# Taking one step of look-ahead and two row buffers out of a software-pipelined attention loop

## The reference

```
p = softmax(q k^T * scale + bias, causal)      # per head, 128 queries at a time
o = p v
```

## Time and profile before

| | us |
|---|---|
| median of 3 runs | 2262.34 |
| lowest, highest | 2261.17, 2263.99 |
| profiled execution, its own time | 2263.99 |
| its span in the trace | 2262.7 |
| PE busy | 2133.4 (94%) |
| DVE, ACT, POOL busy | 988.6, 815.3, 226.7 |

### The profile page before, as it was taken

The page is one execution under the profiler, slowest core; times in us unless marked ns, Lnnn a source line. Parts: engine busy times, 40 slices in busy tenths (PEclk is TensorE's granted clock), DMA queues, the critical chain, the costliest instruction groups (busy, mean ns, idle before and its releaser), DMA issues. The chain is left out here.

```text
span 2262.7 us, 25574 instructions
## 1 busy us (share of the span) xinstructions
PE 2133.4 (94%) x10364; PEld 1712.6 (76%) x10364; DVE 988.6 (44%) x1833; ACT 815.3 (36%) x1574; POOL 226.7 (10%) x256
## 2 busy tenths in 40 slices
PE   6899899999998999999999999988898999999997
PEld 5667688888887767688888877767665788888886
DVE  6265453323336364453323346645355444333333
ACT  4145443223224355342222334342355434222222
POOL 3003410000000004210000000000254201000000
PEclk9899999999999999999999999989899999999999
DMA  6521123233332312123333222313411232323321
GB/s 154 109 75 57 57 80 106 89 98 103 93 98 71 94 47 75 62 84 97 98 98 93 98 80 75 93 29 84 103 48 38 61 117 84 102 89 101 100 89 69
DMA packets 273721, 192.10 MB, mean 85 GB/s; under 512 B 22060, under 2 KB 241364, under 8 KB 273604
## 3 DMA queue, kind: packets, MB, share of 16 engines
q1 hardware_dynamic: 268704, 177.76, 27.3%
q0 software_dynamic: 4752, 12.67, 2.5%
q10 hardware_dynamic: 148, 0.04, 0.0%
HBM read 186.21 MB, written 4.23 MB: 84 GB/s over the span
## 5 line engine op out<-in xcount | busy, mean ns | idle before, releaser
L584 PE MATMUL bank<-h_features,weights_hi_lo 128*128 128x512 f32 (+1 forms) x5160 | 1138.2, 381 | 17.1 <-DVE weights_hi_lo L917 7.9
L584 PEld LDWEIGHTS bank<-h_features,weights_hi_lo 128*128 128x128 f32 x5160 | 933.7, 190 | 206.7 <-issue 14.6
L917 DVE TENSOR_TENSOR weights_hi_lo<-weights,weights_hi_lo 128x1024 fp32r<-128x1024 f32 (+1 forms) x337 | 402.7, 1199 | 703.7 <-ACT weights_hi_lo L1521 703.1
L1521 ACT ACTIVATE weights_hi_lo<-weights 128x1024 fp32r<-128x1024 f32 (+1 forms) x337 | 340.9, 1016 | 401.2 <-PE bank L626 352.4
L624 PE MATMUL bank<-weights_hi_lo,hidden 128*128 128x512 f32 x528 | 205.4, 389 | 0.0
L625 PE MATMUL bank<-weights_hi_lo,hidden 128*128 128x512 f32 x528 | 205.4, 389 | 0.0
L626 PE MATMUL bank<-weights_hi_lo,hidden 128*128 128x512 f32 x528 | 205.4, 389 | 0.0
L1637 ACT ACTIVATE hidden<-arena 128x512 fp32r<-128x512 f32 x66 | 41.7, 632 | 300.0 <-DVE arena L1068 300.0
L1930 POOL TENSOR_SCALAR arena<-arena,row_stats 128x256 f32<-128x256 f32 (+5 forms) x140 | 126.3, 913 | 198.7 <-DVE row_stats L992 70.9
L1902 POOL TENSOR_TENSOR h_features<-arena,h_features 128x512 fp32r<-128x512 f32 x24 | 30.7, 1278 | 992.0 <-ACT h_features L1549 992.0
L1068 DVE TENSOR_TENSOR arena<-bank,arena 128x512 f32<-128x512 f32 x66 | 45.6, 692 | 181.3 <-PE bank L584 181.3
(11 more groups left out here) (335 smaller groups left out, 2063.8 us busy)
## 6 DMA issues: line engine op xcount, KB each, us to landing
weights<-in_w_in_dram SPq DMA_DIRECT2D x84, 512.0 KB, 3.9
weights<-in_w_gate_dram SPq DMA_DIRECT2D x66, 512.0 KB, 3.8
weights<-in_w_up_dram SPq DMA_DIRECT2D x66, 512.0 KB, 3.8
weights<-in_w_down_dram SPq DMA_DIRECT2D x60, 512.0 KB, 3.6
weights<-in_w_out_dram SPq DMA_DIRECT2D x24, 512.0 KB, 3.7
bias_rows<-decay_scratch POOLq DMA_DIRECT2D x16, 256.0 KB, 4.0
weights<-in_w_cmp_dram SPq DMA_DIRECT2D x16, 256.0 KB, 5.4
weights<-in_w_down_dram SPq DMA_DIRECT2D x12, 256.0 KB, 2.6
```

The source lines that it names most:

```text
L584: last = e.matmul(out_ap, l, r, start=(j == 0), stop=(j == len(pairs) - 1))
L917: e.tensor_tensor(pair_view(i, 1), raw_view(i), pair_view(i, 0).bitcast(F32), ALU.subtract).then_inc(done, tick(("split", i)))
L1521: e.activation(pair_view(i, 0), raw_view(i), ACT.Copy).then_inc(done, tick(("hi", i)))
```

## The change

`LAG`, the number of iterations after the last step, goes from 6 to 5. The transposes of a step and their copies come two iterations after its scores instead of three, the values and their output one iteration earlier too. The row buffers shrink from eight to six, so a step reuses the rows of step i-3. `HEAD_AT` and `HEAD_OUT_AT` move one iteration earlier; the other fills stay at their iterations. The same edit is made in the loops of all engines.

```diff
-LAG = 6
-HEAD_AT = {4 * h + 10: h for h in range(N_DIFF)}
-HEAD_OUT_AT = {4 * h + 22: h for h in range(N_DIFF)}
+LAG = 5
+HEAD_AT = {4 * h + 9: h for h in range(N_DIFF)}
+HEAD_OUT_AT = {4 * h + 21: h for h in range(N_DIFF)}
...
-        ATTN_E = [arena(12288 + 512 * i, T) for i in range(6)] + [arena(16384, T), JUNK[:, :]]
+        ATTN_E = [arena(12288 + 512 * i, T) for i in range(6)]
...
-        NSA_E = [arena(8192 + 512 * i, T) for i in range(6)] + [arena(12288, T), TOK_WORDS[:, 1024:1536]]
+        NSA_E = [arena(8192 + 512 * i, T) for i in range(6)]
...
-                        if 3 <= i <= n + 2:
-                            turn_weights(steps[i - 3], [rows[(2 * (i - 3) + j) % 8] for j in range(2)])
-                        if i - 4 in groups:
-                            weigh_values(groups[i - 4])
+                        if 2 <= i <= n + 1:
+                            turn_weights(steps[i - 2], [rows[(2 * (i - 2) + j) % 6] for j in range(2)])
+                        if i - 3 in groups:
+                            weigh_values(groups[i - 3])
...
-                                    if i >= 4:
-                                        dve.wait_ge(*row_free(steps[i - 4], j))
+                                    if i >= 3:
+                                        dve.wait_ge(*row_free(steps[i - 3], j))
...
-                        if i - 5 in groups and groups[i - 5].final:
-                            g = groups[i - 5]
+                        if i - 4 in groups and groups[i - 4].final:
+                            g = groups[i - 4]
```

More of the change, by code:

```diff
@@ L965, in attend @@
                     n = len(steps)
-                    row = lambda i, j: rows[(2 * i + j) % 8]
+                    row = lambda i, j: rows[(2 * i + j) % 6]
                     for i in range(n + LAG):
@@ L1000, in attend @@
                         fill(i)
-                        if 3 <= i <= n + 2:
-                            u = steps[i - 3]
+                        if 2 <= i <= n + 1:
+                            u = steps[i - 2]
                             for j in range(len(u.turned)):
@@ L1564, in attend @@
                                 if u.bias is None:
-                                    if i >= 4:
-                                        act.wait_ge(*row_free(steps[i - 4], j))
+                                    if i >= 3:
+                                        act.wait_ge(*row_free(steps[i - 3], j))
                                     bank = banks[*u.name, "s", j]
@@ L1591, in attend @@
                                     banks.leave(act, (*u.name, "turned", j))
-                        if i - 4 in groups and groups[i - 4].final:
-                            g = groups[i - 4]
+                        if i - 3 in groups and groups[i - 3].final:
+                            g = groups[i - 3]
                             if s == "M" or g.tile >= N_DIFF:
@@ L1928, in attend @@
                                 for j in range(2):
-                                    row = rows[(2 * (i - 1) + j) % 8][:, 0:u.w]
+                                    row = rows[(2 * (i - 1) + j) % 6][:, 0:u.w]
                                     e.tensor_scalar(row, row, st[:, 6 + j:7 + j], None, ALU.mult).then_inc(done, tick((*u.name, "scaled", j)))
```

## The result

The changed kernel takes 2301.2 us (median of 4 runs, 2294.0 to 2307.5) against 2262.9 (4 runs, 2261.2 to 2264.0): it is 38 us slower and not 13, the direction as forecast and the time outside the range. The ratio is 1.0162, interval 1.0135 to 1.0190; it takes in three more runs of the changed kernel (2295.1, 2297.2 and the profiled one, 2303.4), so by it the loss is nearer to 37 us. The profiled execution of it spans 2302.1 us, 39.4 more than the one before.

A forecast was written before the change was run, and what follows sets the result against it. The prediction took PE, busy 94% of the span, to bound the kernel. It added 11.2 us for M and 2.2 for L0 and L1, 13.4 in all, to the median of 2262.3: 2275.7 us, range 2262 to 2285.

The forecast's parts named there:

- the total, 11.2 + 2.2: Whole kernel: 11.2 us lost in M plus 2.2 in L0 and L1, 13.4 us slower, 2275.7 us.
- The second mis-sized term: Loops of L0 and L1: a loss of 1.1 us a layer, 2.2 in both.
- Row buffers at nothing: Six row buffers instead of eight: the wait for a free row is always over when reached, cost 0.
- M's idle time: M's loop: 3.2 + 4.6 + 0.5 + 0 at repeating gaps, 1.3 at its beginning, 1.6 at its end, 11.2 us.
- Kinds B and C: M's iterations 8, 20, 32, 44 (B: new gap replaces old, cost 0) and 12, 24, 36 (C: loss 3.2 us).
- Kind A: M's iterations 4, 16, 28, 40: transposes wait 1.2 us more for POOL's rows, four times, 4.6 us in sum.
- The signs: Trace checks: M's transposes wait 8 to 14 us for POOL, M's loop some 170 us, L0's 160; clock under 0.88 means wrong.
- the third rival: M's clock falls more often, seven more slow stretches of 1.5 us, 2287 us; or row buffers are scarce; chance 12%.
- T(10): Transposes of step 10 in L0 and L1, at iteration 12 between two fills: wait 1.8 us for a mix on DVE.
- The drain: L0 and L1 after the last fill: last scores end 4.2 us later, following chain 8.3 instead of 11.6, loss 0.9.
- Rival 1, faster: Products with the values fill PE's gaps and no transposes wait: about 2252 us, chance 7%.
- Rival 2, hidden anyway: New waits just take the place of old ones, only the loops' ends count: 2262 to 2266 us, chance 19%.

The follow-up runs named there:

- five other traces: Short distance in M alone (2284.1 us); changed kernel with eight row buffers (2302.8), old head-square iterations (2295.6), short POOL scaling in L0 and L1 (2296.0), earlier fox fills (2292.5).
- the control: Kernel before, with 60 unread products in M's loop ahead of transposes where no gap follows: 2272.7 us, ratio 1.0062.

## Why the prediction was wrong

The direction held, and so did the mechanism of M: turns that come too early wait for their rows. The size did not. The step that failed is the total, 11.2 + 2.2: it adds idle time alone and holds no term for the lower clock that the gaps bring, 16.6 us of M in the profiled execution and 10.3 to 11.3 in five other traces. The second mis-sized term is that of L0 and L1, 2.2 us in the sum and 12.9 in the trace. Point by point:

- *Row buffers at nothing*: right, 2302.8 against 2301.2.
- *M's idle time*, forecast +11.2: +8.2 measured. Kinds B and C are in the trace as worked out: T(23) and T(24) wait 1.8 us between them, and POOL's wide rows come 1.56 us apart. Kind A was put at 1.2 four times. T(28) waits 0.94 for its first half, T(16) 0.74, T(4) 0.22 and T(40) not at all.
- *The signs*: over the whole loop PE waits 14.3 us for POOL at L668, just above the band of 8 to 14. Waits for L1822 were to stay near 8 and those for L1428 to fall towards 0; they went from 7.6 to 3.9 and from 5.8 to 3.2. My own kinds say why: two of the four gaps of kind A, which stay, stand behind each sort of tile. M's loop took 184.5 us and not some 170, L0's 165.9 and not 160. The clock fell under 0.88 in the changed kernel's trace, which was the sign for the third rival.
- *The clock*: left out of the sum and made a rival of 12%. I took the clock in M at its old 0.92 and costed only idle time. It fell to 0.84, and 16.6 of the 24.8 us of M are busy time at the lower level. One place to see it was the earlier trace rows: M's loop already ran 26 us at half speed. Another was kind A itself. I took S(30) there at 0.85 us, its time at the higher level, where the trace of the kernel before shows 1.65 for it, right behind the gap. A sum that adds gaps to such a loop has to price the clock with them: here 1.3 to 2 times the 8.2 us of idle time added, on top of it. The Trainium skill's page "TensorE: Matmul & The Clock Gate", section "A second HAM failure mode: psum-queue depth-cycling", describes a kernel that cycles through PSUM banks, in which short idle times between groups of matmuls make the clock switch back and forth (the prediction names the section ahead of it). The trace agrees: slow stretches follow gaps of 0.5 to 1.8 us.
- *L0 and L1*, forecast +1.1 a layer: the loops are 7.1 and 5.9 us longer in the trace, and 17.0 in all with the short distance there alone. Here I mis-sized a chain of small terms, nearly all to the same side. My list of L0's waits also left out 1.4 us for POOL's scaling that the old drain had already. PE in order of time in L0 of the changed kernel shows the largest:

```profile
176.39 0.90 PE L668 MATMUL bank<-shape_consts,arena 128*128 128x128 f32 x3 [2.57 <-DVE arena L1017]
...
210.10 1.13 PE L652 MATMUL bank<-arena 64*128 64x512 f32 x4 [0.77 <-ACT gain_row L1703]
...
217.65 0.49 PE L652 MATMUL bank<-arena 64*128 64x128 f32 x4 [0.25 <-ACT arena L1695]
...
272.52 0.52 PE L668 MATMUL bank<-shape_consts,arena 128*128 128x128 f32 x3 [2.41 <-POOL arena L1930]
```

T(10) waits 2.57 and not 1.8. From iteration 13 on I said that nothing waits. But the scores at 16, 20, 24 and 28 read keys that the fill just ahead of them makes (0.25 to 0.5 each for ACT's copy L1695); in the old order V stood between the two. And scores wait for the bank of the head squares three times, not once. That middle part idles 3.3 us where the old one idled 1.2, and I had counted 0.6. The drain cost 2.1 and not 0.9; the 2.41 at 272.52 is T(30) behind POOL.
- *Rival 1, faster*: its half was there. V did fill gaps for a bank (waits for L1428 and L1822 in M fell from 13.4 to about 7), but the second of the wide rows was turned 4.3 to 4.6 us after the scores behind a fill, as I had set against it.
- *Rival 2, hidden anyway*: no.
- *Rival 3, the clock*: this is what happened in M. I priced it at seven stretches more, 11 us. Five traces show 10.3 to 11.3 and that of the changed kernel 16.6; that the time lies above this rival's 2287 too is due to L0 and L1.

Open: what sets the clock beyond the gaps. The same idle time went with 0.84 in one trace and with 0.87 or 0.88 in five, and in the control the same gaps went with 0.95. In L0 and L1, whose clock was 0.98 to 0.99, 5.3 to 6.1 us of new gaps brought only 0.6 to 2.8 us of busy time. The longer drain of L0 and L1 is read from the traces; no run took it away.

## What to carry to other kernels

Before shortening a software pipeline, list for each step when its input is ready, and what the consumer has left to do until then. The latency that counts is that of the slowest engine in the chain (here POOL, two rows in series), not any engine's load. Where a loop's granted clock is already well under 1, as in M (0.92), new gaps can cost more than their length: look for matmuls of one shape at two durations, and price the lower level with the gap. And before comparing two variants by their times, compare the clock in a stretch that neither edit touches. Last, an iteration of distance also separates things that the loop's author never named, like a fill and the scores that read it; such terms are small and add up.

## What the runs showed of the hardware that was not expected

Unread matmuls made the kernel faster. 60 products of 128x512 in gaps of 0.9 to 1.6 us took M's loop from 159.7 to 152.3 us and its clock from 0.92 to 0.98. The same 60 outside gaps raised the clock to 0.95 and the loop to 170.0 us. In the changed kernel 120 of them took M's loop from 184.5 to 170.4 us.
